# Expert down projections: 11 of 112 weight chunks kept in fp32 and multiplied unsplit, from a seventh buffer

## What is computed

```python
def swiglu(h, w_gate, w_up, w_down):
    return (jax.nn.silu(h @ w_gate) * (h @ w_up)) @ w_down

def moe_swiglu(h, router, w_gate, w_up, w_down):
    logits = (h @ router).astype(jnp.float32)
    top_val, top_idx = lax.top_k(logits, TOP_K)
    ...
    for e in range(N_EXPERTS):
        out = out + gates[..., e:e + 1] * swiglu(h, w_gate[e], w_up[e], w_down[e])
```

## Time and profile before

| | |
|---|---|
| median of 3 runs | 2726.74 us (2719.15 to 2737.47) |
| the profiled execution's own time | 2714.44 us |
| its span | 2712.3 us |
| mean granted TensorE clock | 0.98 |
| read from HBM | 524.9 MB |

### The profile page before, as it was taken

One profiled execution on the slowest core, in us unless ns is written; L12 is line 12 of the kernel. 1 busy time (PEld: TensorE's weight loads), 2 busy tenths in 40 slices (PEclk: granted clock), 3 DMA queues, 4 the chain that ended last, 5 costly groups with the idle time before them and its releaser, 6 DMA issues.

```text
span 2712.3 us, 68677 instructions
## 1 busy us (share of the span) xinstructions
PE 2469.7 (91%) x30242; PEld 2044.9 (75%) x30250; DVE 1898.1 (70%) x2256; ACT 1601.2 (59%) x2162; POOL 355.6 (13%) x180
## 2 busy tenths in 40 slices
PE   6998999999999999989999999978989899898987
PEld 6766766778767777766667877778888888888887
DVE  6666564335355566676643354489999999999998
ACT  5454345343453344534453334578888888888886
POOL 0000001000000000000020000013243323332331
PEclk9999999999999999999999999999999999999999
DMA  6411221133446444211311333389999999999996
GB/s 220 148 48 49 64 63 41 59 106 111 139 154 217 157 149 121 93 49 33 94 32 41 109 117 124 124 306 388 385 387 391 388 383 385 385 389 386 385 389 230
DMA packets 304056, 531.43 MB, mean 196 GB/s; under 512 B 18544, under 2 KB 145776, under 8 KB 303376
## 3 DMA queue, kind: packets, MB, share of 16 engines
q1 hardware_dynamic: 303616, 525.99, 55.0%
q10 hardware_dynamic: 144, 1.05, 0.1%
HBM read 524.91 MB, written 2.10 MB: 194 GB/s over the span
## 4 chain that ended last, share of the span: by engine, by line
PE 51%; DVE 34%; ACT 8%; issue 6%; DMA 0%; POOLq 0%; POOL 0%; ACTq 0%; DVEq 0%; SPq 0%
DVE arena L3011 24%; PE bank L898 10%; PE bank L749 5%; PE bank L1419 4%; PE bank L1372 4%; PE bank L779 3%; PE bank L1435 2%; DVE yacc L3019 2%; PE bank L918 2%; PE bank L859 2%; PE bank L869 2%; PE bank L688 2%; PE bank L783 1%; PE bank L791 1%; PE bank L1523 1%
## 5 line engine op out<-in xcount | busy, mean ns | idle before, releaser
L3011 DVE TENSOR_TENSOR arena<-ring,arena 128x2048 bf16<-128x2048 f32 x334 | 829.5, 2528 | 1.3 <-ACT arena L2229 1.3
L2229 ACT ACTIVATE arena<-ring 128x2048 bf16<-128x2048 f32 x334 | 636.9, 1912 | 96.2 <-DMA ring<-in_moe_w_down 26.7
L1523 PE MATMUL bank<-arena 128*128 128x0 bf16 x10752 | 494.3, 210 | 97.6 <-DVE arena L3011 92.3
L1523 PEld LDWEIGHTS bank<-arena 128*128 128x128 bf16 x10752 | 482.1, 100 | 110.4 <-DVE arena L3011 100.2
L1673 POOL TENSOR_TENSOR arena<-yacc,arena 128x512 bf16<-128x512 f32 x112 | 298.4, 2675 | 957.3 <-ACT arena L2252 957.3
L898 PE MATMUL bank<-feat,ring 128*128 128x256 f32 x1408 | 366.3, 398 | 10.0 <-ACT arena L1735 4.9
L898 PEld LDWEIGHTS bank<-feat,ring 128*128 128x128 f32 x1408 | 256.7, 194 | 73.0 <-issue 26.2
L1540 PEld LDWEIGHTS bank<-arena 128*128 128x128 bf16 x5376 | 238.1, 98 | 21.2 <-issue 20.2
L1540 PE MATMUL bank<-arena 128*128 128x0 bf16 x5376 | 245.0, 206 | 6.3 <-issue 4.3
L1742 ACT ACTIVATE arena<-bank 128x256 f32<-128x256 f32 (+1 forms) x164 | 72.6, 443 | 209.4 <-PE bank L749 85.6
L1650 POOL TENSOR_TENSOR arena<-arena 64x512 f32<-64x512 f32 x16 | 22.4, 1401 | 1022.9 <-ACT arena L1882 857.0
(11 more groups left out here) (402 smaller groups left out, 3998.7 us busy)
## 6 DMA issues: line engine op xcount, KB each, us to landing
ring<-in_moe_w_gate SPq DMA_DIRECT2D x112, 1024.0 KB, 8.3
ring<-in_moe_w_up SPq DMA_DIRECT2D x112, 1024.0 KB, 7.7
ring<-in_moe_w_down SPq DMA_DIRECT2D x112, 1024.0 KB, 8.2
ring<-in_w_in SPq DMA_DIRECT2D x76, 1024.0 KB, 5.2
ring<-in_xa_w_kv SPq DMA_DIRECT2D x16, 1024.0 KB, 5.7
ring<-in_ffn_w_gate SPq DMA_DIRECT2D x11, 1024.0 KB, 5.3
ring<-in_ffn_w_up SPq DMA_DIRECT2D x11, 1024.0 KB, 5.8
ring<-in_ffn_w_down SPq DMA_DIRECT2D x11, 1024.0 KB, 6.0
```

The lines of the kernel that those rows point to most:

```text
L1523: m = mm(o, w[k // 4][wi][:, k % 4, col:col + P], xg[:, e % 2, xi, k, :].shape_from_register(width[e % 2]), start=i == 0 and k == 0, stop= ...
L2229: sc.activation(w_parts[b][0], ring[:, b * FFN_SLOT:(b + 1) * FFN_SLOT], ACT.Copy).then_inc(S["w_hi"], 1)
L3011: v.tensor_tensor(w_parts[b][1], ring[:, b * FFN_SLOT:(b + 1) * FFN_SLOT], w_parts[b][0], ALU.subtract).then_inc(S["w_lo"], 1)
```

## The change

Of the 112 down chunks the 11 with `h` = 1 and n % 5 == 2 (n = 2, 7, ..., 52) are "whole". A whole chunk

- lands in a seventh slot (`whole_slot`, behind the six, inside the same `ring` tensor; own semaphore `slot6`). Its issue waits until TensorE has used the whole chunk before it, and not for `w_lo`;
- gets no `hi` and no `lo`, and takes no part of the rotation of `ring` and `w_parts`; the chunks behind it move up by one place;
- is multiplied by 16 fp32 matmuls over all 256 columns, with the fp32 hidden values in `sil`, in place of 48 bf16 matmuls over the expert's width. `down` then waits for `slot6` and `mo_act` (the product) in place of `w_lo` and `mo_al`. GpSimd's subtraction and ScalarE's rounding of these hidden values fall away.

Since whole products add to all 256 columns of the PSUM tiles, the first matmul of each output tile of an expert (8 for each expert) is now over all 256 columns too. The waits that count events are counted anew (`splits`, `PART_USED`). How the weights lie in HBM is kept.

```diff
-        def part_free(c):
...
+        def whole(n, h):
+
+            return h == 1 and n % 5 == 2
...
+        WHOLE = [n for n in range(NE * STEPS) if whole(n, 1)]
+        whole_slot = view(ring, 6 * FFN_SLOT, FFN_SLOT)
+        PART_USED = [used(0, i) for i in (1, 1, 3, 3)]
+        for n in range(1, NE * STEPS):
+            PART_USED += [used(n, i) for i in (1, 1, 3, 3, 4, 5)[:5 if whole(n - 1, 1) else 6]]
...
+            def load_down(n):
+
+                (dst0, src0), (dst1, src1) = down_chunks(n, n // STEPS)
+                load_moe([(dst0, src0)])
+                if not whole(n, 1):
+                    load_moe([(dst1, src1)])
+                    return
+                k = WHOLE.index(n)
+                if k:
+
+                    sp.wait_ge(S["mo_used"], used(WHOLE[k - 1] + 1, 5))
+                sp.dma_start(whole_slot, src1).then_inc(S["slot6"], 16)
...
-                    load_moe(down_chunks(n - 1, (n - 1) // STEPS))
-            load_moe(down_chunks(NE * STEPS - 1, NE - 1))
+                    load_down(n - 1)
+            load_down(NE * STEPS - 1)
...
-                    w = part_of(2, D)
                     pair = 2 * n + h
-                    pe.wait_ge(S["mo_al"], pair + 1)
+                    if whole(n, h):
+                        w, products = view(ring, 6 * FFN_SLOT, 2, D), ((None, None),)
+                        pe.wait_ge(S["slot6"], 16 * (WHOLE.index(n) + 1))
+                        pe.wait_ge(S["mo_act"], pair + 1)
+                    else:
+                        w, products = part_of(2, D), PASSES
+                        pe.wait_ge(S["mo_al"], splits(pair + 1))
...
-                        o = bk(3 + d // 2, (d % 2) * T, T).shape_from_register(width[e % 2])
+                        all_ = bk(3 + d // 2, (d % 2) * T, T)
+                        o = all_.shape_from_register(width[e % 2])
                         for j in range(2):
-                            for i, (wi, xi) in enumerate(PASSES):
...
+                            for i, (wi, xi) in enumerate(products):
+                                first = f == 0 and h == 0 and j == 0 and i == 0
+                                lhs = (w if wi is None else w[wi])[:, j, d * P:(d + 1) * P]
+                                rhs = sil[:, pair % 4, j, :] if xi is None else act_parts[xi][:, 2 * (pair % 4) + j, :]
+                                if not first and xi is not None:
+                                    rhs = rhs.shape_from_register(width[e % 2])
+                                m = mm(all_ if first or xi is None else o, lhs, rhs,
...
             for q in range(2 * NE * STEPS):
-                pool.wait_ge(S["mo_ah"], q + 1)
+                if whole(q // 2, q % 2):
+                    continue
+                pool.wait_ge(S["mo_ah"], splits(q + 1))
...
-                    if q >= 4:
-
-                        act.wait_ge(S["mo_al"], q - 3)
+                    if q >= 4 and not whole(q // 2 - 2, q % 2):
+
+                        act.wait_ge(S["mo_al"], splits(q - 3))
...
                     if n:
                         hi()
-                        hi()
+                        if not whole(n - 1, 1):
+                            hi()
...
-                    hidden_hi(2 * n + 1)
+                    if not whole(n, 1):
+                        hidden_hi(2 * n + 1)
...
                     if n:
                         lo()
-                        lo()
+                        if not whole(n - 1, 1):
+                            lo()
```

More of the change, by code:

```diff
@@ L88, in make_consts @@
     return np.concatenate([np.asarray(c[n], np.float32).reshape(P, w) for n, w in CONSTS], 1)
-SEMS = ("in_dma par_dma mem_dma wl_dma slot0 slot1 slot2 slot3 slot4 slot5 weights_used "
+SEMS = ("in_dma par_dma mem_dma wl_dma slot0 slot1 slot2 slot3 slot4 slot5 slot6 weights_used "
         "dve_step act_step norm_ss norm_ms norm_sd rout_dma norm_xn norm_x0 norm_r norm_T feat_ready feat_half x_new "
@@ L500, in ff_slot, with splits @@
             return (n + (4 if n < 3 * (FF // 256) else 1)) % FFN_BUFS
-        def part_free(c):
-            c -= FFN_BUFS
-            n, i = (0, c) if c < 4 else ((c - 4) // 6 + 1, (c - 4) % 6)
-            return used(n, (1, 1, 3, 3, 4, 5)[i])
+        def whole(n, h):
+            return h == 1 and n % 5 == 2
+        def splits(q):
+            return sum(not whole(p // 2, p % 2) for p in range(q))
+        WHOLE = [n for n in range(NE * STEPS) if whole(n, 1)]
[3 more added lines that the diff above has]
+            PART_USED += [used(n, i) for i in (1, 1, 3, 3, 4, 5)[:5 if whole(n - 1, 1) else 6]]
         SIDE = {(1, 0): ("y", 0), (1, 1): ("y", 1), (1, 2): ("y", 2), (2, 0): ("y", 3), (2, 1): ("w", 0),
@@ L1536, in down @@
                     for d in range(KT):
-                        o = bk(3 + d // 2, (d % 2) * T, T).shape_from_register(width[e % 2])
+                        all_ = bk(3 + d // 2, (d % 2) * T, T)
+                        o = all_.shape_from_register(width[e % 2])
                         for j in range(2):
-                            for i, (wi, xi) in enumerate(PASSES):
-                                m = mm(o, w[wi][:, j, d * P:(d + 1) * P],
-                                       act_parts[xi][:, 2 * (pair % 4) + j, :].shape_from_register(width[e % 2]),
+                            for i, (wi, xi) in enumerate(products):
[5 more added lines that the diff above has]
+                                m = mm(all_ if first or xi is None else o, lhs, rhs,
                                        start=f == 0 and h == 0 and j == 0 and i == 0 and d % 2 == 0,
-                                       stop=f == STEPS - 1 and h == 1 and j == 1 and i == 2 and d % 2 == 1, skip_group_check=True)
+                                       stop=f == STEPS - 1 and h == 1 and j == 1 and i == len(products) - 1 and d % 2 == 1,
+                                       skip_group_check=True)
                         if pair == 2 * NE * STEPS - 1 and d % 2:
@@ L2225, in hi @@
                     if made[0] >= FFN_BUFS:
-                        act.wait_ge(S["mo_used"], part_free(made[0]))
+                        act.wait_ge(S["mo_used"], PART_USED[made[0] - FFN_BUFS])
                     made[0] += 1
@@ L2315, in moe @@
                     side(n, 1)
-                    hi()
+                    if more or not whole(n, 1):
+                        hi()
                     hidden_hi(2 * n)
@@ L3074, in moe @@
                 lo()
-                lo()
+                if not whole(NE * STEPS - 1, 1):
+                    lo()
                 for t in range(TT):
```

## The result

The changed kernel takes 2729.69 us (median of 20 runs, 2722.76 to 2744.39) against 2721.22 us (median of 20 runs) for the kernel before: a ratio of 1.003, 95% interval 1.0017 to 1.0044. It is slower by 8 us, where 10 us faster was forecast. The time lies within the stated range of 2699 to 2733 us, the sign is the other one.

The account below looks back on a forecast made before the run. It took the expert stage as a balance: VectorE 100% busy, DMA 1 to 3% below its limit. VectorE would allow 32 us, DMA 10, TensorE costing nothing: 2726.7 - 10 = 2716.7 us, range 2699 to 2733 us.

Parts of the forecast that it names:

- VectorE's saving: Expert stage: 11 splits and their stretch beside GpSimd's subtractions fall away, VectorE needs 31.8 us less (25 to 36).
- DMA's room: Expert stage: how much faster chunks can flow than 386 GB/s; 0 to 24 us, taken as 10 us.
- The likeliest case: Expert stage: part of VectorE's gain comes through, 3 to 24 us, about 2703 to 2724 us; chance 0.56.
- The rival that VectorE's gain comes through in full: Expert stage: DMA can follow at 400 GB/s on average, 32 us go, 2695 us; chance 0.10.
- TensorE's term: Whole down products: 16 fp32 matmuls take 3.6 us, 1.55 us more than a split chunk, 17 us in all.
- Cost on the path: nothing: TensorE's extra 1.55 us per whole chunk fits into the 1.85 us a step has without work; otherwise up to 22 us.
- the slower rival: End of step n + 1: TensorE becomes the bound every fifth step, 24 to 36 us over 11, 2757 us; chance 0.08.
- its "if": Slower rival's condition: 24 to 36 us are lost only if the four steps between whole chunks don't make it up.
- The signs that were named: Profile after, 1800 to 2660 us: VectorE near 97%, idle ended by ScalarE's L2229, 387 to 394 GB/s, landings over 8.1 us.

Follow-up runs that it names:

- e1: Changed kernel with each of the 11 whole chunks multiplied over only its first 128 of 256 hidden features; stage 905.8 us, ratio 0.9979 to the kernel before.
- e2: Changed kernel with each whole chunk multiplied by one fp32 matmul in place of 16; stage 905.4 us, ratio 0.9983 to the kernel before.
- e4: Kernel before with VectorE's split of the same 11 down chunks cut to 64 of 2048 columns; stage 906.2 us, ratio 0.9971.
- e5: Kernel before with VectorE's splits from the seventh chunk on cut to 1024 of 2048 columns; stage 904.4 us, ratio 0.996.
- e9: Kernel before with splits halved from the seventh chunk on and gate and up chunks loaded from w_down in 4 KB runs; stage 873.7 us, ratio 0.9878.
- e7: Changed kernel with one fp32 matmul per whole chunk and gate and up chunks loaded in 4 KB runs; stage 895.7 us, ratio 0.992 to the kernel before.
- e3: Kernel before with 168 narrow matmuls in place of 48 on TensorE at the same 11 places; stage 938.3 us, ratio 1.0058.

## Why the prediction was wrong

**VectorE's saving: right.** 31.8 us forecast, 32.3 measured on the page.

**DMA's room: right in mechanism and nearly in size.** The likeliest case took 10 us between bounds of 0 and 24. With TensorE's price away, e1 and e2 gain 7.5 to 7.9 us, e4 7.1, and with VectorE far from the bound e5 gains 8.9. The rival that VectorE's gain comes through in full is excluded for 2 KB runs, and e9 shows that their rate is what excludes it. With 4 KB runs e7 gets 17.6 of the 32 us, so TensorE's waits would have kept a part even then.

**TensorE's term: mis-sized, and this made the sign.** The sum had 16 x 0.224 = 3.6 us for a whole product; it takes 6.91, or 7.07 with the last one's pipeline. The 0.224 us was the price of a record, and I multiplied it by the 16 matmuls of the code. What was then called covered, "Cost on the path: nothing", cost 13.5 us. The row itself held the factor: L1283 has 32 records for a layer, and in the code that line runs for 4 heads x 2 row tiles x 2 parts = 16 matmuls a layer. The term was 11 x (6.91 - 2.04) = 54 us and not 17, and the 4.87 us of a whole chunk don't fit into the 1.85 us that a step has free, but pass it by 3.0. The point from which the slower rival decides, 3.9 us, was given right, and its price of 6.1 to 7.2 us a chunk holds the measured 6.9 to 7.1, though it was put down to matmuls that don't overlap or a low clock. Neither is the case: 32 records in 6.91 us are 0.216 us each while a record lasts 0.379 us, so they do overlap, and the clock was granted in full (1.00) at the place shown.

**What the lateness costs: less than the rival said.** It gave 24 to 36 us over 11 places. The runs give 13.5 us, 1.2 us a place, from the 905.5 us that DMA would allow. The four steps between make up part of it, as its "if" said. The same comes out of the places alone. The whole product at the first and the eleventh place, in the changed kernel and then in e1:

```profile
1838.75 7.14 PE L1572 MATMUL bank<-yacc,ring 128*128 128x256 f32 x32
2666.09 7.14 PE L1572 MATMUL bank<-yacc,ring 128*128 128x256 f32 x32
```

```profile
1850.95 3.69 PE L1572 MATMUL bank<-yacc,ring 128*128 128x256 f32 x16
2665.74 3.69 PE L1572 MATMUL bank<-yacc,ring 128*128 128x256 f32 x16
```

The ten stretches from one place to the next took 827.3 us in the changed kernel and 814.8 in e1, 12.5 us less. Single stretches differ by anything from -1.1 to 3.0 us, so 1.2 us a place is a mean. Now what happens there. Busy times of the changed kernel for the 21 us before one whole product and the 26 us from it on, and the same at another place:

```profile
2064.00:2085.00 21.00, 20.92 (x404) 18.59 (x402) 19.80 (x15) 15.26 (x12) 1.16 (x1) 1.00 1.04 393
2085.00:2111.00 26.00, 25.92 (x446) 24.53 (x446) 24.41 (x13) 22.16 (x20) 6.72 (x4) 1.00 1.03 378
2146.00:2167.00 21.00, 19.96 (x413) 19.15 (x411) 20.30 (x13) 15.66 (x16) 3.19 (x1) 1.00 1.04 391
2168.00:2194.00 26.00, 26.00 (x363) 21.70 (x362) 21.79 (x14) 19.55 (x16) 7.05 (x4) 1.00 1.00 369
```

Before the place DMA runs at 391 to 393 GB/s, better than in the kernel before; behind it TensorE works without a gap for 26 us, VectorE waits for its product, slots come free late, and DMA falls to 378 and 369 GB/s. These are two of the four places with the deepest fall. Over the first ten places DMA's mean is 392 GB/s in the 21 us before, 384 in the 26 us from the place on and 378 in the 35 us after that; e1 has 392, 389 and 388 there. In those last 35 us VectorE is busy throughout, so what it lost behind the place it has no idle time to win back. Taken together: 7.5 to 8 us gained up to DMA's ceiling, 13.5 us lost behind the 11 places, 5.7 us slower in the stage, and 8 us by the medians.

In e3, where VectorE had no slack of its own, nearly the same lateness (5.1 us) cost 2.3 us a place; with the 2.9 us that a whole chunk takes from VectorE it cost 1.2. This fits VectorE's saving having worked as a buffer against TensorE, but it compares two kernels by one trace of e3, and no run shows it alone.

**The signs that were named.** VectorE under 100% came true (96%), ScalarE's waits for landings rose from 62.6 to 75.4 us, and the median landing from 8.1 to 9.4 us. But VectorE's idle time was to be ended by ScalarE's rounding, and most of it was ended by TensorE: 26 of 36 us from 1800 to 2680, against 8.6 for the rounding. The GB/s were to rise to 387 to 394 and fell to 384; with waits for TensorE behind the whole product, that is the slower case as it was described.

## What to carry to other kernels

When the DMA is nearly full beside an engine at 100%, taking load from that engine is worth only the distance to the next ceiling, here 8 us of 32; measure that ceiling first, by cutting the busiest engine's work everywhere. Take a duration and its count from the same place: a price per record of the trace goes with records, and the code's loop count has to be checked against the count in the row. Work that is moved onto an engine with 11% idle costs its lateness at that place, and where it is put in the order decides who stands still behind it.

## What the runs showed of the hardware

- An fp32 matmul of 128x128 weights by 256 columns is two records of 0.216 us each, 0.43 us together, against 0.0425 us for a bf16 one over an expert's columns.
- Loads of 1 MiB into all partitions sustain 390 GB/s over 700 us with two thirds of the bytes in 2 KB runs and the rest in 4 KB runs, and 403 GB/s with 4 KB runs alone, side by side in HBM (e5, e9). In e5 a packet of 2 KB took a median 86 ns and one of 4 KB 162 ns. The DMA share was 1.04 and 1.02: the share doesn't tell the two rates apart.
- More chunks in flight than three don't raise the rate: the median time to landing went from 8.1 to 12.8 us in e5, for 0.8% more GB/s.
- The longest of VectorE's full splits took 3.25 to 3.28 us in every kernel whose splits weren't halved, against a median of 2.28 us. At 323 splits and 101 subtractions of GpSimd the splits lasted 797.2 - 323 x 2.281 = 60 us longer than by their median, in place of 68.3 at 334 and 112.
